# Second attention stage of a two-block layer kernel: order of the row blocks, joined score products, place of the compressed branch

## The reference

```python
def attend_block(args):                      # i = 0..3, 128 queries each
    qi, i = args
    t = i * Q_BLOCK + jnp.arange(Q_BLOCK)
    s_c = jnp.einsum('bhgqd,bhnd->bhgqn', qi, kc) * scale
    p_c = masked_softmax(s_c, c_end[None, :] <= t[:, None])
    o_c = jnp.einsum('bhgqn,bhnd->bhgqd', p_c.astype(vc.dtype), vc)
    ...
    s_s = jnp.einsum('bhgqd,bhgqkd->bhgqk', qi, k_g) * scale
    p_s = masked_softmax(s_s, valid[:, :, None])
    ...
    s_w = jnp.einsum('bhgqd,bhkd->bhgqk', qi, k_wi) * scale
    p_w = masked_softmax(s_w, m_w)
    ...
out = (gates[..., 0:1] * unblock(o_c) + gates[..., 1:2] * unblock(o_s)
       + gates[..., 2:3] * unblock(o_w))
```

## Time and profile before

| what | us |
|---|---|
| median of 3 runs | 2815.89 (2810.91 to 2831.61) |
| the profiled execution | 2822.58 |
| its span, first to last instruction | 2820.8 |
| TensorE busy in the span | 2672.4 (95%) |
| VectorE, ScalarE, POOL busy | 1506.9, 989.5, 456.8 |

### The profile page before, as it was taken

One profiled execution on the slowest core, in us unless ns is written; L12 is line 12 of the kernel. 1 busy time (PEld: TensorE's weight loads), 2 busy tenths in 40 slices (PEclk: granted clock), 3 DMA queues, 4 the chain that ended last, 5 costly groups with the idle time before them and its releaser, 6 DMA issues.

```text
span 2820.8 us, 32969 instructions
## 1 busy us (share of the span) xinstructions
PE 2672.4 (95%) x13540; PEld 2170.3 (77%) x13540; DVE 1506.9 (53%) x2346; ACT 989.5 (35%) x1450; POOL 456.8 (16%) x474
## 2 busy tenths in 40 slices
PE   7999999999999979999999989999798999999998
PEld 3888888879888878966888778888577554588786
DVE  4765455367777777367622465535543442443444
ACT  4212111246555653134422342323322233343343
POOL 0101000114544361000000000001001431020110
PEclk8999999999999999998999999999996689999999
DMA  7444454313111112020222233333224311222221
GB/s 295 154 183 176 172 193 178 148 62 126 64 49 68 49 71 94 16 90 1 103 91 90 90 117 125 123 120 140 85 68 119 87 46 60 104 94 99 97 86 43
DMA packets 58247, 294.59 MB, mean 104 GB/s; under 512 B 14705, under 2 KB 19953, under 8 KB 30193
## 3 DMA queue, kind: packets, MB, share of 16 engines
q1 hardware_dynamic: 56944, 282.52, 27.4%
q10 hardware_dynamic: 1152, 9.96, 0.9%
HBM read 271.75 MB, written 20.71 MB: 104 GB/s over the span
## 4 chain that ended last, share of the span: by engine, by line
PE 80%; DVE 10%; ACT 6%; issue 2%; POOL 1%; DMA 1%; SPq 0%; DVEq 0%; POOLq 0%; ACTq 0%
PE ps L314 79%; DVE wl L926 1%; POOL rp L2952 1%; DVE hd L1572 1%; PE ps L3101 1%; ACT x L1527 1%; ACT wh L917 0%; DVE x L1606 0%; DMA x<-in_x 0%; ACT hd L1511 0%; DVE t L955 0%; ACT hd L1509 0%; DVE hd L1574 0%; ACT L675 0%; DVE at L1624 0%
## 5 line engine op out<-in xcount | busy, mean ns | idle before, releaser
L314 PE MATMUL ps<-xs,wh 128*128 128x512 f32 (+1 forms) x2816 | 785.9, 366 | 17.8 <-DVE xs L960 13.8
L314 PEld LDWEIGHTS ps<-xs,wh 128*128 128x128 f32 x2816 | 509.4, 190 | 105.3 <-issue 16.7
L314 PE MATMUL ps<-xs,wl 128*128 128x512 f32 (+1 forms) x1408 | 513.5, 365 | 0.0
L314 PE MATMUL ps<-h,wh 128*128 128x512 f32 (+1 forms) x1408 | 391.0, 364 | 8.0 <-POOL h L1159 8.0
L910 DVE TENSOR_TENSOR wl<-w,wh 128x2048 fp32r<-128x2048 f32 (+4 forms) x114 | 244.2, 2143 | 257.5 <-ACT wh L904 257.3
L904 ACT ACTIVATE wh<-w 128x2048 fp32r<-128x2048 f32 (+4 forms) x114 | 204.5, 1794 | 325.0 <-PE ps L314 274.2
L314 PEld LDWEIGHTS ps<-xs,wl 128*128 128x128 f32 x1408 | 267.6, 190 | 42.2
L314 PEld LDWEIGHTS ps<-h,wh 128*128 128x128 f32 x1408 | 253.5, 189 | 51.4 <-POOL h L1159 9.7
L314 PE MATMUL ps<-x1h,wh 128*128 128x512 f32 x584 | 240.8, 412 | 26.3 <-DVE at L1624 16.9
L314 PE MATMUL ps<-h,wl 128*128 128x512 f32 (+1 forms) x704 | 255.8, 363 | 0.0
L314 PE MATMUL ps<-x1lr,wh 128*128 128x512 f32 x584 | 235.5, 403 | 0.0
(11 more groups left out here) (452 smaller groups left out, 4453.1 us busy)
## 6 DMA issues: line engine op xcount, KB each, us to landing
w<-in_adat SPq DMA_DIRECT2D x52, 1024.0 KB, 5.0
w<-in_f1i SPq DMA_DIRECT2D x22, 1024.0 KB, 6.4
w<-in_f2i SPq DMA_DIRECT2D x22, 1024.0 KB, 4.8
w<-in_f3i SPq DMA_DIRECT2D x22, 1024.0 KB, 4.8
s_tables<-t ACTq DMA_DIRECT2D x4, 2368.0 KB, 8.2
w<-in_ada SPq DMA_DIRECT2D x8, 1024.0 KB, 9.1
w<-in_whf SPq DMA_DIRECT2D x8, 1024.0 KB, 4.8
w<-in_whqg SPq DMA_DIRECT2D x8, 1024.0 KB, 4.8
```

The source lines that it names most:

```text
L314: return e.matmul(out, l, r, start=st, stop=sp)
```

## The change

Three things change in the one list and in the functions that walk it.

The order of row blocks becomes `AO = (3, 0, 2, 1)`: in the first 16 steps pairs of heads of row block 3 (512 keys) and row block 0 (128 keys) alternate, in the second 16 row blocks 2 (384) and 1 (256). The buffers for sums and gates are now indexed by the step and not by the head.

Where W is at most 256, the scores of both branches are one product (2W columns, into the same bank as before).

The compressed branch of row block `AO[0]` no longer stands ahead of step 0: its three parts come behind steps 0, 1 and 2, those of the second behind 3, 4 and 5, of the third behind 14, 15 and 17, of the fourth behind 18, 19 and 20. Two pairs' output banks (`val`) are now in use at a time, and `combine` stands at two even steps of each eight.

```diff
-    AU = [(n // 8, n % 8, 128 * (n // 8 + 1)) for n in range(32)]
+    AO = (3, 0, 2, 1)
+    AP = [(AO[2 * (p // 8) + p % 2], p % 8 // 2) for p in range(16)]
+    AG = [(AO[2 * (g // 4) + g % 2], g % 4 // 2) for g in range(8)]
+    AU = [(i, 2 * q + h, 128 * (i + 1)) for i, q in AP for h in range(2)]
...
-        out = [("comp", 0, s) for s in range(3)]
-        for n in range(36):
+        out = []
+        comps = {0: (0, 0), 1: (0, 1), 2: (0, 2), 3: (1, 0), 4: (1, 1), 5: (1, 2),
+                 14: (2, 0), 15: (2, 1), 17: (2, 2), 18: (3, 0), 19: (3, 1), 20: (3, 2)}
+        for n in range(37):
...
-            if n >= 6 and n % 4 == 2:
-                out.append(("combine", (n - 6) // 4))
+            if n >= 4 and n % 2 == 0 and (n - 4) // 2 % 4 >= 2:
+                p = (n - 4) // 2
+                out.append(("combine", p // 4 * 2 + p % 2))
...
-            if n < 24 and 3 <= n % 8 <= 5:
-                out.append(("comp", n // 8 + 1, n % 8 - 3))
+            if n in comps:
+                out.append(("comp", *comps[n]))
...
             elif item == "scores":
                 i, h, W = AU[n]
+                if W <= 256:
+                    b = rows(banks.take(w, "sc2", n, 0)[:, 0:2 * W], 2)
+                    mm(e, b, q8[0:64, h, 128 * i:128 * i + 128], k2[0:64, :, h // 4, 0:W], True, True).then_inc(*scP.of(n, 1))
+                    continue
                 for y in range(2):
-                    if y == 0 or W > 256:
-                        banks.take(w, "sc2", n, y)
+                    banks.take(w, "sc2", n, y)
                     mm(e, scores(n, y), q8[0:64, h, 128 * i:128 * i + 128], k2[0:64, y, h // 4, 0:W], True,
                        True).then_inc(*scP.of(n, y))
...
-                H = n // 2
-                i, kv = H // 2, H % 2
-                if n % 2 == 0:
-                    banks.take(w, "val", H)
+                i, q = AP[n]
+                kv = q // 2
+                if q % 2 == 0:
+                    banks.take(w, "val", i, kv)
```

More of the change, by code:

```diff
@@ L2807, in b2_items @@
                 out.append(("turned", n - 2))
-            if n >= 4 and n % 2 == 0:
+            if n >= 4 and n % 2 == 0 and (n - 4) // 2 < 16:
                 out.append(("values", (n - 4) // 2))
@@ L2905, in act_att @@
                         if n > 1:
-                            w.wait_ge(*vlP.at(4 * n - 5))
+                            w.wait_ge(*vlP.at(n + 4))
                         e.activation(PCT[n % 2][0:31, 512 * h:512 * h + 512], banks("ct", n, h)[0:31, :],
@@ L2910, in act_att @@
                 i, h, W = AU[n]
-                H = n // 4
                 w.wait_ge(*mxV.at(n, "min", 1))
@@ L2919, in act_att @@
                                  bias=C2M[n % 4][:, y:y + 1],
-                                 accum_out=SUM[H % 2][:, y, h % 4:h % 4 + 1]).then_inc(*exA.of(n, y))
+                                 accum_out=SUM[n // 4 % 2][:, y, n % 4:n % 4 + 1]).then_inc(*exA.of(n, y))
             elif item == "turned":
@@ L2951, in pool_att @@
                     p = PB[(2 * n + y) % 4][:, 0:W]
-                    e.tensor_tensor(p, p, RS[(n // 4) % 2][:, y, h % 4:h % 4 + 1].to_broadcast([128, W]),
+                    e.tensor_tensor(p, p, RS[n // 4 % 2][:, y, n % 4:n % 4 + 1].to_broadcast([128, W]),
                                     ALU.mult).then_inc(*wtG.of(n, y))
@@ L2975, in dve_att @@
                 if s == 0:
-                    cm = cst2("cmask").rearrange("p (i n) -> p i n", i=4)[:, n, :].unsqueeze(1).to_broadcast(wide)
+                    cm = cst2("cmask").rearrange("p (i n) -> p i n", i=4)[:, AO[n], :].unsqueeze(1).to_broadcast(wide)
                     w.wait_ge(*cmP.at(n, "s"))
@@ L2995, in dve_att @@
                     w.wait_ge(*cmV.at(n, "inv"))
-                    tt(r, r, gv[:, n, :, 0], ALU.mult).then_inc(*cmV.of(n, "gate"))
+                    tt(r, r, gv[:, AO[n], :, 0], ALU.mult).then_inc(*cmV.of(n, "gate"))
                     w.wait_ge(*cmV.at(n, "gate"))
@@ L3020, in dve_att @@
                 i, h, W = AU[n]
-                r, q = [z[(n // 4) % 2][:, :, h % 4:h % 4 + 1] for z in (RS, SUM)]
+                r, q = [z[n // 4 % 2][:, :, n % 4:n % 4 + 1] for z in (RS, SUM)]
                 w.wait_ge(*exA.at(n, 1))
@@ L3029, in dve_att @@
             elif item == "combine":
-                i, kv = n // 2, n % 2
-                b = banks("val", n)[0:64, :].rearrange("p (k o t) -> p k o t", k=2, o=2)
-                w.wait_ge(*vlP.at(2 * n + 1))
+                i, kv = AG[n]
+                b = banks("val", i, kv)[0:64, :].rearrange("p (k o t) -> p k o t", k=2, o=2)
+                w.wait_ge(*vlP.at(4 * (n // 2) + n % 2 + 2))
                 for o in range(2):
@@ L3070, in pe_att @@
                     for h in range(8):
-                        m = mm(e, b[:, 31 * h:31 * h + 31], q8[0:64, h, 128 * n:128 * n + 128],
+                        m = mm(e, b[:, 31 * h:31 * h + 31], q8[0:64, h, 128 * AO[n]:128 * AO[n] + 128],
                                KC[0:64, 31 * (h // 4):31 * (h // 4) + 31], True, True)
@@ L3105, in pe_att @@
             elif item == "values":
-                H = n // 2
-                i, kv = H // 2, H % 2
-                if n % 2 == 0:
-                    banks.take(w, "val", H)
[L3110 to L3113, removed]
+                i, q = AP[n]
+                kv = q // 2
+                if q % 2 == 0:
+                    banks.take(w, "val", i, kv)
+                c = slice(256 * (q % 2), 256 * (q % 2) + 256)
+                o = banks("val", i, kv)[0:64, c]
+                w.wait_ge(*cmA.at(AO.index(i), "t", kv))
+                mm(e, o, VC[0:31, 64 * kv:64 * kv + 64], PCT[AO.index(i) % 2][0:31, 512 * kv + c.start:512 * kv + c.stop], True, False)
                 w.wait_ge(*tnA.at(2 * n + 1, 1))
@@ L3121, in pe_att @@
             elif item == "combine":
-                banks.give(("val", n), (cbV, n, 1))
+                banks.give(("val", *AG[n]), (cbV, n, 1))
             elif item == "in":
```

## The result

The changed kernel takes 2843.59 us (median of 4 runs, 2837.79 to 2845.6), the kernel before 2813.4 (4 runs). The ratio is 1.0098, 95% interval 1.0063 to 1.0132: slower by about 28 us, 1%. The profiled execution took 2845.31, 22.7 more than that of before.

The account below looks back on a forecast made before the run. Attention was taken as bound by TensorE's work, low clock and idle. Forecast 147.8 + 68 + 27 = 243 us against 220.7, 22 more, gave 2844.7 profiled, 2838 as median, rounded to 2836; range 2797 to 2860.

Parts of the forecast that it names:

- Stage: Second block's attention: 147.8 work at 2.4 GHz, 68 lost to low clock, 27 idle, 243 us against 220.7.
- the 4 us that the prediction took off: Second half of attention: 8-record value runs may raise the clock by themselves, cutting its loss from 72 to 68 us.
- Low clock: Attention at 1.2 GHz for 157 us, 12 of them idle, so 72 us lost, taken as 68.
- Idles: TensorE waits for POOL at heads 10, 14, 18, 22, 26, 30; stage idle 27 us against 20.
- 1.2 + 2 + 1.8: VectorE's SSM products and scans ahead of the minima at steps 9, 17 and 23: 5 us more idle.
- Start: Moving the compressed chain gains no idle time: 4.5 us idle before u,cs in place of 3.7 + 0.7.
- Joined scores: For 16 narrow heads, halving the score pieces at 0.09 us overhead each was taken to save 1.7 us.
- Drain: At the end of attention: 1 us of idle.
- The difference in medians: Whole kernel: 2844.7 us profiled, less 6.7 for the median, gives 2838, rounded to 2836.
- The third rival: Idles at width changes don't lower the clock; stage 189 us, 31 us faster, 2785; chance 0.13.
- the first: Rival: attention's low stretches come out no longer than before; 5 us slower, 2821; chance 0.22.
- the second: Rival: once low, the clock finds no run long enough to rise; low 220 us, +50 us, 2866; chance 0.20.

Follow-up runs that it names:

- the pads: Changed kernel with 25 products that nobody reads, over 128 rows, put where TensorE idles: 0.9949 of the kernel before, 2806.89 us.
- the swap: Changed kernel with the inverse sums of head n-1 listed ahead of the minima of head n: 0.9980 of the kernel before, 2811.74 us.
- the part alone: Kernel before with only the first compressed softmax moved behind steps 0, 1 and 2: ratio 0.9985.
- joined products alone: Kernel before with only the joined score products: ratio 1.0001 to the kernel before.
- the start's pads of 64 rows: Changed kernel with unread products where TensorE idles, contracting over 64 rows in place of 128: 0.9996 of the kernel before, 2815.85 us.
- the padded kernel before: Kernel before with 18 unread products put where TensorE idles: ratio 0.9940, 2800.6 us.
- the swap alone: In the plain order: kernel before with the inverse sums of head n-1 listed ahead of the minima of head n: ratio 0.9949, 2805.41 us.
- the other idles padded too: Changed kernel with inverse sums ahead of minima, plus unread products where it still idled: 0.9919 of the kernel before, 2795.27 us.
- the kernel before with swap and pads: Kernel before with inverse sums ahead of minima, plus unread products where TensorE idles: ratio 0.9955, 2808.43 us.
- the order alone: Changed kernel without the joined product and with the first compressed softmax ahead of step 0 again: 1.0099 of the kernel before.

## Why the prediction was right

The median was forecast at 2836 (2797 to 2860) and came to 2843.6, slower by 0.98% where 0.7% was forecast, and "within 1%" was only just right. Against the profiled execution the sum gave 2844.7 and the trace 2845.3. Term by term:

- **Stage.** 243 forecast, 241.9 measured, split 147.8 + 68 + 27 against 147 + 71 + 24. The three errors are of 1 to 3 us and cancel, which is luck in part. Without the 4 us that the prediction took off for rises at runs of eight value records, its 72 would have met the 71: of three such runs begun at 0.50, those at 2306.05 and 2357.08 brought no rise and that at 2336.16 ended at 1.0. The mechanism (idles at the width changes, most followed by a long low stretch) is shown: by the rows after, by the pads (-37 us with work added) and by the swap (-32 us with nothing added or left out).
- **Low clock.** 157 us forecast, 155 measured (153.6 stretch by stretch). Up to step 18 the course is the forecast's: 31, 20, 31 and 27 us against 31, 20.5, 27 and 31, but for one break: the clock rose for some 3 us at 2158, which it wasn't expected to do before the values of step 4 (below). Behind steps 22, 24, 26 and 30, 7 + 4 + 24 + 13 stand against 24, nothing of its own, 3.4 and 17: the places were wrong, and the sums, 48 and 44, are near each other by luck.
- **Idles.** Six places forecast, six found. Steps 22, 26 and 30 have 1.9, 1.3 and 1.2 us against 2.1 each, and step 18 3.7 against 4.1; step 14 has 2.06 against 2.7 (the profile puts its end down to ScalarE's exponentials, L2924, but in the kernel the turning waits for POOL's product, which started at 2232.37). Step 10 has 5.4 us against 3.9: item `y`'s wait for its DMA, ahead of the minima on VectorE, was not in the sum, and explains 1.0 us of the 1.5 at most. The mis-sized term is "1.2 + 2 + 1.8": over the 2.7 and 2.1 us of their steps the SSM's items cost 2.7 at step 10 and 1.6 at step 18, and behind step 23 only 0.16 us of wait stands.
- **Start.** "This part gains no idle time": 4.35 us against 4.5 forecast, and the part alone has 0.9985 (0.9958 to 1.0011).
- **Joined scores.** This step was wrong: "0.09 a piece is overhead". The time lies on the group and not on the record, and the gain of 1.7 us is 0. (Stretch by stretch the work term is 148.0 us before, 147.6 with joined products alone and 146.6 in the changed kernel.)
- **Drain.** 1 us was set for the end. The next stage's first product waits 1.56 us for ScalarE (L3168, the GELU and its table), which 16 records of values covered before and 8 don't.
- **The difference in medians** is 30 us, in profiled executions 22.7. The profiled execution of before was one of its slower ones, which the prediction said (6.7 above the median) but it took the same 6.7 us off the changed kernel, whose profiled execution was 1.7 above its median. That step makes 5 us of the 7.6 between 2836 and 2843.6; the rounding from 2838 makes 2 more.

The third rival, idles that are harmless, fell: filled, the kernel gains 37 us. So did the first, low stretches no longer than before (154 us against 113), and the second: the clock was back at 1.0 in or right behind each of the six runs of twelve or sixteen value records that began at 0.50. The rule weighed in the prediction (the Trainium skill, page "TensorE: Matmul & The Clock Gate", section "Why this matters for your kernels"), that keeping TensorE busy gives it full clock, isn't borne out: 16 us at 0.50 over the start's pads of 64 rows and the u,cs behind them, and 44 in the padded kernel before, with TensorE busy throughout.

## What to carry to other kernels

Read the granted clock beside every wait of TensorE: an idle of 2 to 4 us was followed here by low stretches that cost up to 14 us (30.6 us at 0.50, 28.55 of it busy, behind the 3.66 of step 18; 27.3 behind the 2.06 of step 14), and two list items swapped so that a short VectorE product no longer stood behind the next head's minima gave back 32 us. Before mixing wide and narrow work to even out the load, check what the in-order engines have to do between the narrow piece and the wide one's next step. An order is best judged after such waits are taken away, and all of them: with the swap alone the plain order was still ahead of the alternating one by 6 us, with the other idles padded too it was behind by 13.

## What the runs showed of the hardware that was not expected

The clock also rises without a run of value products. In the changed kernel it did so near 2158, after eight turnings and eight compressed transposes; in the kernel before with swap and pads near 2169, within transposes and the SSM's output products:

```profile
2165.89 1.91 PE L3084 MATMUL ps<-cst,t 128*31 128x128 f32 x8
...
2169.18 0.39 PE L314 MATMUL ps<-xs,cs 128*128 128x64 f32 x2
```

A pair of xs,cs records takes 0.63 us up to 2168.8 and 0.39 from 2169.2. So "only value runs bring it back" is too narrow. Before these rises TensorE worked on products over 128 rows, but that alone doesn't bring the clock back: u,cs, 32 records over 128 rows, runs for 7.09 us at 0.50 four times in the traces of the two kernels, the clock staying low behind it each time.

Nor does the work just before settle it. In the kernel before and in the same kernel with the swap, TensorE does the same from 2161 to 2173 without a gap, at the same speed and within 0.1 us of the same times, and the clock rises in the second only, at 2173.6; in the first it stays low for 50 us more. What differs is the wait ahead, at the turning of head 1 (2.58 us and 1.50). First the kernel before, then the one with the swap:

```profile
2172.25 0.52 PE L314 MATMUL ps<-xs,cs 128*128 128x64 f32 x2
...
2173.85 0.63 PE L314 MATMUL ps<-xs,cs 128*128 128x64 f32 x2
```

```profile
2172.34 0.53 PE L314 MATMUL ps<-xs,cs 128*128 128x64 f32 x2
...
2173.77 0.39 PE L314 MATMUL ps<-xs,cs 128*128 128x64 f32 x2
```

The clock also falls without an idle. In the kernel before it falls at 2264.3, behind compressed scores and SSM products, after TensorE had been busy without a gap since 2252.95, and stays low for 10.2 us:

```profile
2252.95:2264.30 11.35, 11.35 (x62) 0.85 0.12 48
```

The 0.85 of this row is a low stretch of 3.4 us, over at 2257.4. So idles lower the clock here, but not only idles, and what else does isn't shown.

Useless work can make a kernel faster: 25 unread products in the changed kernel took 37 us off.

The kernels differ in spread: the order alone varied by 1.3 us over 4 runs, the kernel before by 21 over 4 runs and by 30 over 25, the padded kernel before by 26. The spread is one of the clock: over the 89 runs of the kernel before that were timed beside the trials, the fastest (2804.6 us) has a mean granted clock of 0.965 and the slowest (2834.6) one of 0.954, and the two go together closely (correlation -0.98). Why the same kernel gets another clock from run to run was not tested; that idles of about 1 us sometimes lower it and sometimes don't is a guess.
